# A decoder layer on one core: two weight loads of the output projection are queued behind a copy of the rotary key rows

## The reference

```
h = x @ w_in[l]
(qa, ka, va, ga, iq, ik, iw, c_q, c_kv, k_rope, gb) = _split_cols(h)
...
o_a = _dsa_branch(qa, ka, va, iq, ik, iw) * jax.nn.silu(ga)
o_b = _mla_branch(c_q, c_kv, k_rope, q_norm_g[l], w_uq[l], kv_norm_g[l],
                  w_ukv[l], positions) * jax.nn.silu(gb)
out = jnp.concatenate([o_a, o_b], axis=-1) @ w_out[l]
x = _layernorm(DEEPNORM_ALPHA * x + out, ln_g[l], ln_b[l])
```

## Time and profile before

| | |
|---|---|
| time, median of 3 runs | 309.57 us (309.50 to 309.86) |
| time of the profiled execution | 309.57 us |
| its span, first to last instruction | 307.7 us |
| TensorE busy | 294.7 us, 96% of the span |
| VectorE busy | 235.3 us, 76% |
| ScalarE busy | 170.9 us, 56% |
| GpSimd busy | 158.7 us, 52% |
| mean granted clock of TensorE | 0.995 of full speed |

### The profile page before, as it was taken

The page is one execution under the profiler, slowest core; times in us unless marked ns, Lnnn a source line. Parts: engine busy times, 40 slices in busy tenths (PEclk is TensorE's granted clock), DMA queues, the critical chain, the costliest instruction groups (busy, mean ns, idle before and its releaser), DMA issues.

```text
span 307.7 us, 5163 instructions
## 1 busy us (share of the span) xinstructions
PE 294.7 (96%) x1646; PEld 253.4 (82%) x1646; DVE 235.3 (76%) x540; ACT 170.9 (56%) x411; POOL 158.7 (52%) x180
## 2 busy tenths in 40 slices
PE   7979999999999999999999999999999999999990
PEld 7969988888888888888889789998677777888890
DVE  1959967888999999996043644855789998987785
ACT  5843274575242262374357787998867885554200
POOL 4869855303999975535326697820492010335211
PEclk9999999999999999999999999999999999999998
DMA  7947442200434532320058333230950000040411
GB/s 253 342 129 207 136 139 71 68 2 0 117 91 136 154 112 78 102 68 2 0 136 205 140 137 117 90 62 8 350 192 0 2 0 3 0 137 2 136 68 68
DMA packets 14777, 31.24 MB, mean 102 GB/s; under 512 B 1728, under 2 KB 4288, under 8 KB 14752
## 3 DMA queue, kind: packets, MB, share of 16 engines
q1 hardware_dynamic: 14192, 30.60, 32.6%
q10 hardware_dynamic: 560, 0.33, 0.4%
HBM read 26.28 MB, written 2.10 MB: 92 GB/s over the span
## 4 chain that ended last, share of the span: by engine, by line
PE 87%; DVE 5%; issue 2%; DMA 2%; ACT 2%; SPq 0%; POOL 0%; DVEq 0%; ACTq 0%; POOLq 0%
PE ps L1067 46%; PE ps L1348 14%; PE ps L1275 6%; PE ps L1225 5%; PE ps L1291 5%; PE ps L1306 3%; PE ps L1216 2%; DMA w_raw<-in_w_in 2%; PE ps L1219 2%; PE ps L1132 1%; DVE x_lo L717 1%; PE ps L1151 1%; PE ps L1320 1%; PE ps L1122 1%; ACT oT L645 1%
## 5 line engine op out<-in xcount | busy, mean ns | idle before, releaser
L403 POOL TENSOR_TENSOR w_lo<-w_raw,w_hi 128x512 fp32r<-128x512 f32 (+3 forms) x62 | 79.3, 1298 | 41.1 <-ACT w_hi L496 41.0
L1067 PE MATMUL ps<-w_hi,x_hi 128*128 128x512 f32 (+2 forms) x220 | 83.2, 378 | 2.9 <-POOL w_lo L403 1.5
L1067 PE MATMUL ps<-w_hi,x_lo 128*128 128x512 f32 (+2 forms) x220 | 82.0, 373 | 0.0
L1067 PE MATMUL ps<-w_lo,x_hi 128*128 128x512 f32 (+2 forms) x220 | 82.0, 373 | 0.0
L496 ACT ACTIVATE w_hi<-w_raw 128x512 fp32r<-128x512 f32 (+3 forms) x62 | 36.2, 591 | 73.3 <-PE ps L1067 72.3
L1067 PEld LDWEIGHTS ps<-w_hi,x_hi 128*128 128x128 f32 x220 | 41.4, 188 | 9.8 <-issue 2.7
L1067 PEld LDWEIGHTS ps<-w_hi,x_lo 128*128 128x128 f32 x220 | 41.3, 188 | 6.5
L1067 PEld LDWEIGHTS ps<-w_lo,x_hi 128*128 128x128 f32 x220 | 41.4, 188 | 5.9
L1348 PE MATMUL ps<-wo_hi,oT 128*128 128x512 f32 (+1 forms) x144 | 44.3, 372 | 0.0
L611 ACT ACTIVATE probs<-probs,small 128x512 f32<-128x512 f32 (+3 forms) x64 | 35.7, 558 | 11.0 <-DVE small L887 10.5
L1275 PE MATMUL ps<-ident,probs 128*128 128x128 f32 x160 | 28.3, 274 | 1.9 <-ACT probs L611 0.9
(11 more groups left out here) (170 smaller groups left out, 557.4 us busy)
## 6 DMA issues: line engine op xcount, KB each, us to landing
w_raw<-in_w_in SPq DMA_DIRECT2D x20, 512.0 KB, 3.6
kaT_swap<-kaT SPq DMA_DIRECT2D x8, 256.0 KB, 3.7
w_raw<-in_w_out SPq DMA_DIRECT2D x4, 512.0 KB, 5.8
wo_early<-in_w_out SPq DMA_DIRECT2D x4, 512.0 KB, 4.2
wo_raw_b<-in_w_out SPq DMA_DIRECT2D x4, 512.0 KB, 5.1
x_res<-in_x SPq DMA_DIRECT2D x4, 512.0 KB, 7.1
w_raw<-in_w_in SPq DMA_DIRECT2D x4, 416.0 KB, 3.7
x_raw<-in_xT SPq DMA_DIRECT2D x3, 512.0 KB, 6.4
```

The costliest lines, as they stand in the source:

```text
L403: pool.tensor_tensor(w_lo[:, s, 0:n], w_raw[:, s, 0:n], w_hi[:, s, 0:n], ALU.subtract).then_inc(w_lo_ready, 1)
L1067: ins = mm(dst, a, b, start=start and j == 0, stop=stop and j == len(pairs) - 1)
```

## The change

Two edits. In SP's list the copy of the key rows comes ahead of the loads of pieces 6 and 7; in POOL's list piece 0 comes ahead of pieces 6 and 7 (`WO_ORDER`).

```
@@ -341,11 +341,11 @@
                 load_early(k)
             sp.wait_ge(acc_ready, A_END + 2)
             load(C_OUT // 2)
-            for k in (6, 7):
-                load_early(k)
             sp.wait_ge(acc_read[2], ACC_LAST[2])
             sp.dma_start(kbT[NOPE:B_QK, 1:B_HEADS, :],
                          kbT[NOPE:B_QK, 0:1, :].broadcast_to([ROPE_D, B_HEADS - 1, SEQ])).then_inc(kpe_copied, 16)
+            for k in (6, 7):
+                load_early(k)
             sp.wait_ge(scores_ready, NU_A)
@@ -1390,7 +1390,7 @@
-WO_ORDER = (1, 2, 3, 4, 5, 6, 7, 0)
+WO_ORDER = (1, 2, 3, 4, 5, 0, 6, 7)
```

## The result

The changed kernel takes **317.02 us** (median of 4 runs, 316.93 to 319.50) against 309.59 us before (309.50 to 309.86). The ratio is 1.0257, with a 95% interval of 1.0208 to 1.0308; it goes by means, which the single run of 319.50 draws up (the medians alone give 1.024). The prediction said 309.9 us, between 309.2 and 310.7, with 0.32 on slower. The place and the first mechanism were right; the price was not.

A forecast was written before the change was run, and what follows sets the result against it. TensorE was taken to bound the kernel, busy 294.7 of 307.7 us. Piece 0 earlier 0, key copy 0 and late loads +0.3 us (0 to +1.2) on 309.57 gave 309.9 us, range 309.2 to 310.7.

The forecast's parts named there:

- the detour: From TensorE's transposes at 208.98 through ACT's and DVE's oT, back on TensorE at 210.44; ACT's copy also needs POOL's casts.
- the zero for piece 0: POOL's casts of piece 0 start at 192.25 instead of 195.99; nobody gains from that, costed at nothing.
- the zero for the key copy: SP still issues the copy at 200.54 after waiting for ACT; landing 9.5 us ahead of first use, it gains nothing.
- POOL beside DVE: A running POOL instruction can hold DVE's gate multiplication up by 0.44 us (1.13 against 0.69 us); cost 0 at both places.
- the row to look for: Sign of being right: ACT's oT names POOL L444 as releaser, or still PE L1320 with a start at 209.06.
- the landing of piece 7: Load of piece 7 behind the key copy lands between 207.61 and 209.03 us, taken as 208.1.
- 205.04 + 1.35 + 1.22: Fast case for piece 7: key copy's landing plus two landing spacings from the stream at 189 us, giving 207.61.
- its wide variant: Piece 7 with the 1.78 us spacing of the stream at 214 us once: 205.04 + 1.78 + 1.28 = 208.10.
- the 0.93 us of the instruction packet: Instruction fetch at about 206.45 us occupies one DMA engine and may delay piece 7 by 0 to 0.93 us.
- I carry it to the end one for one: ACT's late oT delays TensorE's transpose at 210.44 and the end by the same amount, 0.3 us, as nothing takes it up.
- my bound of 1.2: Upper bound of ACT's oT delay: piece 7 at 209.03 plus casts puts its start at 210.3, 1.2 us late.
- rival 1: ACT waits for POOL in earnest: piece 7 lands after 208.4, oT over 0.6 us late, 310.2 to 310.8 us; chance 0.28.

The follow-up runs named there:

- pool_order_only: The kernel before with the new WO_ORDER alone (piece 0 ahead of 6 and 7 on POOL), SP's list as before: 309.96 us, ratio 1.0000.
- filled_gap_9: The changed kernel with 9 unused identity-matrix products in TensorE's list ahead of the waiting transpose: 311.29 us, ratio 1.0054.
- sp_order_only: The changed kernel with the old WO_ORDER, so only SP's order is changed: 318.45 us (two runs, 316.83 and 320.07), ratio 1.0278.
- loads_late_no_copy_ahead: The changed kernel with loads 6 and 7 issued ahead of the key copy, behind the same wait for ACT: 309.94 us, ratio 1.0001.
- act_delay_9: The kernel before with nine useless ACT instructions ahead of ACT's oT copy: 310.5 to 311.1 us in 6 of 10 executions, 313.3 to 316.6 in 4.
- filled_gap: The changed kernel with 18 unused identity-matrix products in TensorE's list ahead of the waiting transpose: 313.60 us, ratio 1.0123.
- act_delay_3: The kernel before with three useless ACT instructions ahead of ACT's oT copy: 310.02 us, ratio 1.0011.
- act_delay_13: The kernel before with 13 useless ACT instructions ahead of ACT's oT copy: 310.9 us in 1 of 7 executions, 313.3 and 316.6 to 317.0 in 6.
- act_delay_18: The kernel before with 18 useless ACT instructions ahead of ACT's oT copy, loads and orders untouched: 317.19 us.

## Why the prediction was wrong, point by point

**Right.** The bound (TensorE full to 209 us), the detour as the place to watch, the zero for piece 0 (`pool_order_only`), and the zero for the key copy, which was issued at 200.55 in the changed kernel as before. POOL beside DVE came out as told: with POOL idle, DVE's L913 took 0.69 us at 196.73 instead of 1.13, and POOL's `vb_parts`, which no longer begins during L913, took 1.27 us instead of 1.67; TensorE had no gap at either place. Also the row to look for, ACT's `oT` released by POOL L444, which stands in the changed kernel with 2.12 us of idle time:

```profile
210.82 0.60 ACT L645 ACTIVATE oT<-ps 128x512 fp32r<-128x512 f32 x1 [2.12 <-POOL wo_hi L444]
```

**Wrong first: the landing of piece 7.** The step was the spacing "205.04 + 1.35 + 1.22", its wide variant, and the 0.93 us of the instruction packet; I took 208.1 and set the bound at 209.03. It landed at 209.56. The copy did land as taken (4.6 us), but piece 6 landed at 207.02 instead of 206.39, and piece 7 2.5 us behind it. Two things in the trace were not in the sum. SP needed 1.94 us to issue piece 7, where all the issues that I had taken the size from took 0.33 to 0.43 us. And at the end, it seems, one DMA engine was left alone: the traffic of the changed kernel from 207.9 to 209.2 us is six packets of 4 KB and a small one, strictly one after the other, with no other packet beside them (first line: mean busy share of the 16 DMA engines in 40 slices).

```profile
DMA  0000000030000300003000030000300030000000
...
DMA packets 7, 0.02 MB, mean 19 GB/s; under 512 B 1, under 2 KB 1, under 8 KB 7
```

The packet of instructions did come in the midst of the two loads (206 to 207 us, row "q8 instruction: 1, 0.02, 5.8%", 0.93 us of one engine), and it fits that one engine was late. In `filled_gap_9` it came between 207 and 208, and piece 7 took 6.7 us instead of 7.3 and 7.6 us in three executions in which it came between 206 and 207, and 7.8 us in one in which it came between 205 and 206. That is what the profiled executions happened to show, not an experiment on it. In the one of 7.8 us (`sp_order_only`) the fetch took longer itself, 9.7% of 16 engines over 1 us, that is 1.55 us. That the copy costs something by itself is shown by `loads_late_no_copy_ahead`: no fetch came before 208 us there, and piece 7 took 6.0 us. The clean comparison is the one above: 4.6 us alone, 7.6 us behind the copy. How much of these 3 us belongs to the copy's own packets, to the held issue and to the instruction packet is not settled.

**Wrong second, and nearly four times as large: "I carry it to the end one for one."** The delay was 1.76 us, above my bound of 1.2, but by my rule that would still have been 311.3 us. Where the clock held, the rule came out, as the start of the transpose (210.44 before) and the span (307.7 before) show: in `act_delay_9` 1.03 us later and 1.0 us longer, in `filled_gap_9` 1.79 and 1.7, in `filled_gap` 3.90 and 3.8. That `filled_gap_9` took just 311.29 is in part chance, since the filling held its transpose. The missing term is the clock. My rival 1 had the mechanism and the point from which it would decide, and priced it with the same rule, 310.2 to 310.8. The row that should have warned me was already in the sum: TensorE would stand still for 0.44 us plus the delay. I asked what else waits behind ACT's copy, and not what an idle TensorE does to its own clock. At the delay that I forecast, 0.3 us, the forecast would even have come true: `act_delay_3`, with 0.28 us, took 310.02 us (ratio 1.0011, 1.0002 to 1.0021). So the price has two parts: one for one with the delay, and on top of it a step that is paid with growing frequency the longer TensorE stands still. A sum with one slope could not show it.

On TensorE's clock the rows say: it held through a standstill of 0.44, 0.71 or 0.77 us in every execution; it fell in some or all executions with 1.27 us or more; it was at half for 13.5 us in the changed kernel, though TensorE was busy throughout them. The Trainium skill, TensorE: Matmul & The Clock Gate, Part 1, has the rule that I had not weighed: the array's clock is gated, throttled is the default, and activity releases it. The trace agrees with it in kind. By that rule a fall of the clock behind the longer standstill was a rival of its own, and I gave it no chance; the runs give its time, some 317 us.

**The range.** It ended at 310.7, because both errors were bounded by rows that showed neither a load behind a copy nor a standstill of this length. I had given slower a chance of 0.32, and slower it was; what was wrong is that nothing above 310.7 was in the range.

## What to carry to other kernels

A wait that holds TensorE is not priced by its length alone: sum up the standstill that it adds to one already there, and where the sum exceeds what has been seen to be harmless (here 0.77 us; at 1.27 us the clock fell in 4 of 10 executions) count a stretch at half clock as well, here some 5.6 us for a delay of 1.8. Before a load is queued behind another transfer, find who waits for what is made from it and how many us are left there; here 12 us of room were given up for an earlier place of a copy that gained nothing by it. And where a wait of that kind can't be avoided, work that nobody needs, or moving the deadline by a few units, is cheaper than letting the engine stand.

## What the runs showed of the hardware

- TensorE's granted clock fell to 0.50 after a standstill of 2.06 to 2.10 us in all executions of two kernels (5 and 4), after 1.64 us in 6 of 7, after 1.27 us in 4 of 10, after 0.77 us in none of 20, after 0.71 us in none of 10 (by the mean clock where there is no trace). The same program on the same chip, `act_delay_9`, took anything from 310.5 to 316.6 us.
- It stayed at half for some 13.6 us of unbroken work in three profiled executions (the changed kernel, `act_delay_13`, `act_delay_18`) and for some 17 us in that of `sp_order_only`, where it fell before TensorE began again.
- A DMA issue on SP that takes 0.33 to 0.43 us took 1.94 us in the changed kernel when it stood behind a copy of 448 KB and a load of 512 KB that were still running.
- A fetch of instructions (16 KB, one packet) took 0.93 us at 206.5 us in the changed kernel and 1.55 us in `sp_order_only`. The last seven packets of piece 7 went through one after the other, with no other packet beside them, and the load landed only behind them.
- A copy of 448 KB within SBUF and two loads of 512 KB took 8.5 to 9.0 us together, three loads of 512 KB 6.1 us.
- DVE's L913 took 1.13 us beside POOL's casts and 0.69 us with POOL idle.
- A product of two 128x128 float32 blocks of the identity matrix stands in the trace as two instructions of about 0.12 us each (18 for 9 products in 2.22 us), where a float32r product here is one.
